# First block of the dilated output projection: its prompt columns multiplied inside the sample attention, its sample columns afterwards

## What is computed

```
def _dilated_mix(h, w_q, w_o, attend):
    q = (h @ w_q).reshape(n, length, N_DIL_GROUPS, HEADS_PER_GROUP, HEAD_DIM)
    for g, (w, d) in enumerate(DIL_PATTERNS):      # (128,1), (512,4), (2048,16)
        o, lse = attend(q[:, :, g], w, d)
        ...
    wts = jax.nn.softmax(jnp.stack(lses), axis=0)[..., None]
    o = jnp.sum(wts * jnp.stack(outs), axis=0).astype(h.dtype)
    return o.reshape(n, length, HEADS_PER_GROUP * HEAD_DIM) @ w_o
```

## Time and profile before

| | us |
|---|---|
| median of 3 runs | 2338.23 (2336.01 to 2339.54) |
| the profiled execution, its own time | 2336.17 |
| its span (first to last instruction) | 2334.4 |
| PE busy in the span | 2313.4 (99%) |
| PEld busy | 2284.4 (98%) |
| DVE, ACT busy | 1333.2, 963.9 |
| granted TensorE clock, mean | 0.998 |

### The profile page before, as it was taken

One profiled execution on the slowest core, in us unless ns is written; L12 is line 12 of the kernel. 1 busy time (PEld: TensorE's weight loads), 2 busy tenths in 40 slices (PEclk: granted clock), 3 DMA queues, 4 the chain that ended last, 5 costly groups with the idle time before them and its releaser, 6 DMA issues.

```text
span 2334.4 us, 46612 instructions
## 1 busy us (share of the span) xinstructions
PE 2313.4 (99%) x19196; PEld 2284.4 (98%) x19196; DVE 1333.2 (57%) x1683; ACT 963.9 (41%) x1153; POOL 105.4 (5%) x126
## 2 busy tenths in 40 slices
PE   9999999999999999999999999999999999999999
PEld 8999998999999999999999998999999999999999
DVE  6778556655545554455646765675554455544554
ACT  7434445433333333334444434553333333333343
POOL 0000112000000000000101022110000000000001
PEclk9999999999999999999999999999999999999999
DMA  8665765555555555555566567655555555555553
GB/s 280 195 194 172 236 206 177 177 179 180 180 180 180 180 179 179 180 178 180 172 194 210 158 195 235 216 164 180 180 180 179 180 179 177 179 178 181 178 171 126
DMA packets 383192, 433.31 MB, mean 186 GB/s; under 512 B 13888, under 2 KB 350096, under 8 KB 382558
## 3 DMA queue, kind: packets, MB, share of 16 engines
q1 hardware_dynamic: 373902, 401.72, 55.1%
q0 software_dynamic: 8464, 29.49, 3.7%
q10 hardware_dynamic: 720, 0.58, 0.1%
HBM read 426.21 MB, written 6.45 MB: 185 GB/s over the span
## 4 chain that ended last, share of the span: by engine, by line
PE 98%; DVE 1%; ACT 1%; DMA 0%; issue 0%; DVEq 0%; SPq 0%; ACTq 0%
PE acc L799 30%; PE acc L801 30%; PE acc L800 30%; PE acc L876 1%; PE acc L877 1%; PE acc L884 1%; PE ab L895 1%; PE ab L1055 0%; PE acc L1010 0%; DMA hA_flat<-in_mem_prompt 0%; PE acc L979 0%; PE acc L989 0%; PE ab L979 0%; PE ab L946 0%; PE ab L1114 0%; PE ab L1092 0%
## 5 line engine op out<-in xcount | busy, mean ns | idle before, releaser
L799 PE MATMUL acc<-xs,whi 128*128 128x264 f32 (+1 forms) x3776 | 1081.1, 286 | 0.3 <-DVE xs L1346 0.3
L801 PE MATMUL acc<-xs,wlo 128*128 128x264 f32 (+1 forms) x3776 | 1073.1, 284 | 0.0
L800 PE MATMUL acc<-xs,whi 128*128 128x264 f32 (+1 forms) x3776 | 1072.2, 284 | 0.0
L477 ACT ACTIVATE whi<-raw 128x1024 fp32r<-128x1024 f32 x744 | 762.5, 1054 | 716.6 <-DMA raw<-in_ffn_w_up 289.3
L1297 DVE TENSOR_TENSOR wlo<-raw,whi 128x1024 fp32r<-128x1024 f32 x744 | 878.2, 1231 | 208.8 <-ACT whi L477 186.6
L801 PEld LDWEIGHTS acc<-xs,wlo 128*128 128x128 f32 x3776 | 713.1, 189 | 0.0
L800 PEld LDWEIGHTS acc<-xs,whi 128*128 128x128 f32 x3776 | 710.7, 188 | 0.3
L799 PEld LDWEIGHTS acc<-xs,whi 128*128 128x128 f32 x3776 | 709.2, 188 | 0.8 <-issue 0.5
L799 PE MATMUL acc<-hA,whi 128*128 128x264 f32 (+1 forms) x1216 | 346.3, 285 | 1.6 <-DVE hA L1584 1.6
L801 PE MATMUL acc<-hA,wlo 128*128 128x264 f32 (+1 forms) x1216 | 345.7, 284 | 0.0
L800 PE MATMUL acc<-hA,whi 128*128 128x264 f32 (+1 forms) x1216 | 345.0, 284 | 0.0
(11 more groups left out here) (297 smaller groups left out, 1163.8 us busy)
## 6 DMA issues: line engine op xcount, KB each, us to landing
raw<-in_ffn_w_gate SPq DMA_DIRECT2D x176, 512.0 KB, 3.5
raw<-in_ffn_w_up SPq DMA_DIRECT2D x176, 512.0 KB, 3.5
raw<-in_ffn_w_down SPq DMA_DIRECT2D x176, 512.0 KB, 3.6
raw<-in_dil_w_q SPq DMA_DIRECT2D x48, 512.0 KB, 3.6
raw<-in_pool_w_in SPq DMA_DIRECT2D x32, 512.0 KB, 3.6
raw<-in_pool_w_out SPq DMA_DIRECT2D x32, 512.0 KB, 3.7
raw<-in_mem_w_v SPq DMA_DIRECT2D x16, 512.0 KB, 6.3
raw<-in_mem_w_k SPq DMA_DIRECT2D x16, 512.0 KB, 4.7
```

The lines of the kernel that those rows point to most:

```text
L477: nc.scalar.activation(half_block(whi, n, half), half_block(raw, n, half), ACT.Copy).then_inc(hi_ready, 1)
L799: mm(out, w_hi, hi_, start=first, stop=False)
L800: mm(out, w_hi, lo_, start=False, stop=False)
L801: return mm(out, w_lo, hi_, start=False, stop=last)
```

## The change

The first item of "do" is taken apart. Two new functions stand in TensorE's program. `prompt_products(n, g, m)` multiplies the 256 prompt columns of one of the two output tiles m, 24 matmuls; it is called for m = 0 behind `dil_turn_keys(7)` and for m = 1 behind `dil_sample_values(0)`. `sample_products(n, g)` adds the products of the 8 sample columns for both tiles, 48 matmuls, and signals `half_used`; it stands where the first item stood. Items 1 to 7 are as before. No other engine's program changes.

```
+            def prompt_products(n, g, m):
+                if m == 0:
+                    item_free(g)
+                    eng.wait_ge(h_ready, hd + NH)
+                for k in range(8):
+                    if k % 4 == 0:
+                        block_ready(n, k // 4)
+                    w_hi, w_lo = (w[:, n % NSPLIT, k * 256 + m * P:k * 256 + m * P + P] for w in (whi, wlo))
+                    out, (h_hi, h_lo) = acc[:, 2 * (g % 2) + m, 0:TP], htile(k, TP)
+                    mm(out, w_hi, h_hi, start=k == 0, stop=False, skip_group_check=True)
+                    mm(out, w_hi, h_lo, start=False, stop=False, skip_group_check=True)
+                    mm(out, w_lo, h_hi, start=False, stop=False, skip_group_check=True)
+
+            def sample_products(n, g):
+                for k in range(8):
+                    for m in range(2):
+                        w_hi, w_lo = (w[:, n % NSPLIT, k * 256 + m * P:k * 256 + m * P + P] for w in (whi, wlo))
+                        out, h_hi, h_lo = acc[:, 2 * (g % 2) + m, TP:T], hA[:, k, 0, TP:T], hA[:, k, 1, TP:T]
+                        mm(out, w_hi, h_hi, start=False, stop=False, skip_group_check=True)
+                        mm(out, w_hi, h_lo, start=False, stop=False, skip_group_check=True)
+                        last = mm(out, w_lo, h_hi, start=False, stop=k == 7, skip_group_check=True)
+                    if k % 4 == 3:
+                        last.then_inc(half_used, 1)
 ...
                 dil_turn_samples(0)
                 dil_turn_keys(7)
+                prompt_products(N0["do"], G0["do"], 0)
                 dil_sample_scores(1)
                 dil_sample_values(0)
+                prompt_products(N0["do"], G0["do"], 1)
                 dil_turn_samples(1)
                 dil_turn_outputs(0)
                 dil_sample_values(1)
 ...
             eng.wait_ge(h_ready, hd + NH + 1)
-            pair_phase("do", 8, 1, htile)
+            sample_products(N0["do"], G0["do"])
+            for j in range(1, 8):
+                pair_item(N0["do"] + j, G0["do"] + j, 1, htile)
```

## The result

| | before | after |
|---|---|---|
| median of 14 runs, us | 2336.53 (2333.65 to 2339.54) | 2342.74 (2340.77 to 2346.56) |
| span of the profiled execution | 2334.4 | 2339.0 |
| mean granted clock | 0.998 | 0.997 |

The ratio is 1.0028, with a 95% interval of 1.0021 to 1.0035: slower by 6.2 us, 0.28%. The two sets of executions don't overlap: the fastest of the kernel after took 2340.77 us, the slowest of the kernel before 2339.54. The mean granted clock was 0.994 to 0.997 in the 14 executions of the kernel after. One execution of the kernel before, measured beside e1 to e4, took 3211 us at a mean clock of 0.653 and is left out of every comparison.

What follows compares the result with a forecast made beforehand. PE, busy 99% of the span, was taken to bound the kernel. Work of +3.1 us and a clock fall of +4.0 us made +7.1 on a median of 2338.23: 2345.3 us, range 2339.5 to 2349.0.

Steps and rivals of the forecast that it cites:

- the work: All added and saved PE work up to the end of item 0, without the clock: +3.1 us.
- the clock: Granted clock falls to 0.50 in the sample products, low about 8 us into item 1: +4.0 us (1.7 to 5.0).
- First prompt products: 24 matmuls ahead of the scores of q = 1, partly covered by PE's wait: scores start +2.11 us later.
- The stop: PE's 1.81 us halt in the sample values of q = 0, read as missing instructions, shrinks: -1.4 us (0 to -1.8).
- Second prompt products: 24 matmuls behind the sample values of q = 0, with no PE wait to cover them: +2.94 us.
- Sample products: In item 0's place, 48 matmuls of 8 columns at weight-load pace, 0.111 us each: 5.33 us, 0.53 shorter than item 0.
- cheap products: Rival for the sample products: weight loads overlap better, 0.066 or 0.027 us each, giving +1.0 or -0.9 us; chance 0.10.
- two passes: Rival for the sample products: each done twice, 0.222 us, and a longer low clock: +14 us, 2352; chance 0.07.
- sum below zero: Rival from the skill's issue gap: 48 sample products at 25 ns take 1.2 us, turning the sum negative; no separate chance.
- Loads: SyncE's load of block 226, at about 1421.5 and needed for item 2 about 7 us later: nothing waits.

Runs made afterwards that it cites:

- e1: Against the kernel before, only the prompt columns of tile m = 0 multiplied early, behind the turn of the last keys; ratio 1.0000.
- e4: The changed kernel with the columns divided 200 early and 64 later; ratio to the kernel before 1.0027.
- e5: The kernel before, loading only the first 64 of 512 channels per group of the cached value rows of samples 4 to 7; ratio 0.9988.
- e2: Against the kernel before, only the prompt columns of tile m = 1 multiplied early, behind the sample values of q = 0; ratio 1.0017.
- e6: The kernel before with 24 transposes of 8x8 added behind the turn of the last keys, where PE waits for ScalarE; ratio 0.9996.
- e3: The changed kernel with the columns divided 136 early and 128 later; ratio to the kernel before 1.0011.
- e7: The changed kernel once more, unaltered, for its trace; one execution, local distance 72.77 us, +7.6 against the kernel before.
- e8: The kernel before, with loads of the cached value rows of samples 6 and 7 held until the last keys are turned; ratio 0.9993.
- e9: The kernel before, with value-row loads of samples 5, 6 and 7 started at the 14th, 15th and 16th turned key item; ratio 1.0002.

## Why the prediction was right

The forecast was +7.1 us, made of +3.1 for the work and +4.0 for the clock, with a median of 2345.3 us and a range from 2339.5 to 2349.0. Locally it is +7.2, the medians differ by 6.2, with an interval from 4.9 to 8.2, and the median is 2342.74 us. Of the 2.6 us by which 2345.3 is too high, 1.7 come from the base: the median of the first three executions of the kernel before was 2338.23, that of all 14 is 2336.53.

**First prompt products.** Forecast +2.11 for the scores, measured +2.20. The 24 matmuls stand 0.118 apart as forecast.

**The stop.** I took -1.4, with -1.8 as the most, so the bound was too narrow. Measured -2.06 in one trace of the change and -1.8 in the other. The mechanism (instructions held up by traffic, PE arriving later) was right and is shown by e5, e1 and e2. The size was off in two ways: the stop costs 2.2 and not 1.81, and next to nothing of it was left, as the piece moved 5.9 us behind the mark instead of 6.4. I had taken the time at which the piece comes as fixed; it came sooner where instructions stood ahead of it (e6).

**Second prompt products.** Forecast +2.94, measured 2.91; nothing covered them.

**Sample products.** Forecast 0.111 each at the full clock. Their first 28 weight loads start (1429.38 - 1426.38)/27 = 0.111 us apart. The rivals with cheap products and with two passes are out. The Trainium skill's rule in TensorE: Matmul & The Clock Gate, section LDWEIGHTS (columns divided by 1.2, 107 ns) agrees at the full clock; at 0.50 the products stand 0.213 us apart. The 25 ns of its section Back-to-back issue gap do not hold here. I had read that section wrongly: it says itself that its table is for the isolated matmul and leaves the weight loads out, so it never spoke for a sum below zero.

**The clock.** Forecast a fall in the sample products, 8 us low, 4.0 lost; measured 10.24 us low. In it lie 21 sample products at 0.213 instead of 0.111 (+2.1) and 26 matmuls of item 1 at 0.220 instead of 0.122 (+2.5): 4.7 us. I had given item 1 3 us at the lower level, and it got 5.7. That few moving columns are the reason is shown by e3 against the change, and e1 fits. The same page's section HAM oscillation names idle gaps as what lowers the clock, and I took it that PE without a gap would keep it; here it fell after 3.0 and 2.6 us of PE busy without a gap.

**Sum.** 2.20 - 2.06 + 2.91 gives 3.05 for the place of item 0 (the trace has 2.99), then 4.7 for the clock and -0.55 for the shorter item: 7.2. The two errors, 0.7 too little taken off for the stop and 0.7 too little put on for the clock, cancelled: that the sum came out within 0.1 us is luck.

**Loads.** Nothing was lost there, as forecast: SyncE starts block 226 at 10.35 us behind the mark instead of 10.21, and from 1432 to 1476 us PE has no wait in the trace.

What the change would have been worth without the fall of the clock is shown nearly by e3: still 2.4 us slower. (Nearly, since e3's early matmuls, of 136 columns, are a little shorter.) The work alone says the same: two prompt groups of 2.94 and 5.33 of sample products stand for 5.86 of item 0, 5.35 us more, and the idle time that they fill is 0.83 + 2.2 = 3.0 us. That leaves +2.3.

## What to carry to other kernels

Dividing matmuls along their moving columns to fill idle time pays only if that time is longer than the weight loads that it doubles: here 0.111 us for each of 48, 5.3 us for 3.0 us of idle time, and 2.7 us for the half that came out even (e1). If columns have to be split off, divide them evenly (136 and 128 here) and not into nearly all and nearly none (256 and 8): in this kernel a run of products with few columns each kept TensorE busy by the profile and still its clock fell, and what came behind paid for it too. And before filling an idle stretch, ask what it is: "issue" in the middle of many small matmuls was a piece of instructions that came late in heavy traffic, and it was gone once TensorE reached that place some 2 us later.

## What the runs showed that I had not expected

The granted clock at the start of the program differs from execution to execution of nearly the same instructions: there is no low stretch near 13 us in the profiles of the change, of e7 and of e8, 3.4 us of it in e2, 6.8 us in before, e1, e3, e4, e6 and e9, and 10.2 us in e5. It explains why the timeline of the change stands 2.4 us ahead of that of before at the mark, and why its span grew by 4.6 us where the local loss is 7.2. The granted clock is also a part of the scatter between executions of one kernel. Of the 21 executions of the kernel before that were measured beside e8 and e9, the four with a mean clock of 1.000 took 2333.69 to 2333.93 us, and those with 0.997 or 0.998 took 2335.77 to 2338.35. What makes it differ was not tried. The start of the kernel after, against the stretch 13.2 to 20.0 of the earlier trace rows:

```profile
10.00:20.00 10.00, 6.82 (x35) 5.45 (x34) 8.79 (x16) 10.00 (x17) 0.00 (x0) 1.00 1.06 395
```

The other surprise is the fall of the clock in e6, with 24 tiny matmuls that stand in a wait and cost nothing themselves.
